# First norm of a decoder layer on one Trainium2 core: row tiles in groups of 2, 4, 4, 4 and 2, half of the squares of x on VectorE, a fifth buffer for raw rows

## The chip, the core and the metric

The kernel runs on one core of a Trainium2 chip. The core has five engines that work side by side, each through its own list of instructions in order, and they wait for each other by semaphores: TensorE (PE, matrix products; its weight loads are PEld), VectorE (DVE), ScalarE (ACT), GpSimd (POOL) and SyncE (SP, which here issues nearly all DMA transfers). The metric is the time of one execution on the device in microseconds, the median of some runs.

## The reference, cut to what matters

One decoder layer on x (512 tokens by 2048 features, fp32): a root-mean-square norm with a shift and scale made from a vector c, a wide projection, two groups of heads (retention, and sparse attention that selects keys by an indexer), an output projection with residual, and an MLP of four times the width behind a second norm. The part that the change touches:

```
def _rms_norm(x, g):
    y = xf * lax.rsqrt(jnp.mean(xf * xf, axis=-1, keepdims=True) + EPS)
    return (y * g.astype(jnp.float32)).astype(x.dtype)
...
    mod = jax.nn.silu(c) @ w_ada + b_ada          # 6 vectors of 2048; w_ada is 2048 x 12288
    shift1, scale1, gate1, shift2, scale2, gate2 = jnp.split(mod, N_MOD, axis=-1)
    h = _modulate(_rms_norm(x, norm1_g), shift1, scale1)   # h * (1 + scale) + shift
    proj = h @ w_in
    ...
    dk = _rms_norm(dk.reshape(B, L, DSA_KV_HEADS, HEAD_DIM), k_norm_g)
```

## The kernel before, in words

All activations lie transposed: a "row tile" kt is 128 features by 512 tokens, 16 of them make h. Every fp32 product is made of three passes over operands split into a high and a low half: ScalarE copies a piece of raw weights to `w_hi` (`split_hi`, L513), GpSimd subtracts to get `w_lo` (`split_lo`, L738), TensorE multiplies (`product`, L1194). Weights come in units of four chunks, numbered q = 4u + j, through two raw slots (`load_unit`, L448).

**Start.** x comes in four tiles of 128 tokens (1 MiB each) through the two halves of `x_nat`; tiles 2 and 3 are fetched when tiles 0 and 1 have been transposed and squared (L464 to L467). TensorE transposes them (`turn_x`), ScalarE copies them to `resid` and squares each with an accumulating sum (L660), all four squares on ScalarE. The four sums give the norm's factor through VectorE, a power on GpSimd (`root`, L747), a spread over partitions on TensorE (L1267) and a copy (L840).

**First norm and first projection.** Shift and scale for 4 row tiles are columns of `silu(c) @ w_ada`. They need 8 pieces of `w_ada` (`first_piece`, L455: 4 of scale, 4 of shift, each 4 x 128 rows by 512 columns, 1 MiB, rows of 2 KB) in four rotating buffers `first`; a piece t of group cc is issued when `first_used` has reached 8 cc + t - 3. TensorE takes a piece with `first_rows` (L1281, 4 products of 32 columns of the array each). After 8 pieces ScalarE copies the sum (`take_first`, L519), TensorE sums it (`sum_first`, L1302), VectorE adds the bias (L815), makes the gain (L820), and with ScalarE's part makes high and low of each row tile (`modulate`, L828 and L832, `h_high`, L523). With row tile kt ready, TensorE runs `early_chunk(kt)`: keys, values and three index tiles of the wide projection. There are four groups of 4 row tiles. In TensorE's order the pieces of group cc stand between the chunks of group cc - 1: none before the first, 4 before the second, 2 before the third, 2 before the fourth, whose middle holds `sum_first(cc)`; after the last pieces of all, chunk 11 to 15 follow.

**What SyncE issues behind that.** After the last piece: the unit of small projections (`U_SMALL`, unit 4); `ada_piece(0)`, which waits until all 32 first pieces have been used (L370); the store of the transposed x, 4 MiB, to `xT_dram` (L485); `ada_piece(1)`, which waits until that store has landed (L372); then unit 5 (`U_IQ`). `resid`'s memory is used again afterwards, so `take_kv` (VectorE, L889) waits for the store too: it takes keys and values of chunk 15 out of PSUM, and TensorE waits for it before its first narrow product of the small unit.

**The keys' norm.** `mean_square` (VectorE) makes the mean squares of the keys, GpSimd takes the power, which in its list stands behind `split_lo` of chunk 20, the first chunk of unit 5 (L767, L751), VectorE scales the keys (`scale_k`, L903), and TensorE transposes them behind the third chunk of the small unit (wait for `k_ready` at L1372).

Further on, pieces of `w_ada` for the other four vectors are summed on VectorE (L1013), and VectorE also adds the index scores (L925).

Of the kernel before, what the change touches and what calls it, by code (L numbers as in the profile page):

```python
# [98 lines left out]


def need(eng, sem, value):

    if isinstance(value, int) and value <= 0:
        return
    eng.wait_ge(sem, value)
# [20 lines left out]
def build(nc, x, vecs, b_ada, consts, w_ada, w_in, w_out, w_mlp1, w_mlp2, out):  # L126
# [21 lines left out]
    def small(name, *shape):  # L148
# [87 lines left out]
    x_turned, x_taken = sem("x_turned"), sem("x_taken")  # L236
    x_squared = sem("x_squared")
    rstd_spread = sem("rstd_spread")
# [117 lines left out]
    for n in range(2, ADA_PIECES):  # L356
        after = max(after, ada_place(n)[2] - 1)
        ADA_AFTER.setdefault(after, []).append(n)

    block = nc.Block()  # L360
    with block:
# [3 lines left out]
        def _(sp):  # L365
            def ada_piece(n):

                (sec, k), (b, _, freed) = divmod(n, 4), ada_place(n)
                if n == 0:
                    sp.wait_ge(first_used, 32)  # L370
                if n == ADA_EARLY[0]:
                    sp.wait_ge(xT_stored, 16)  # L372
                    sp.wait_ge(t_ready, KT)
                if n == ADA_LATE[0]:
                    sp.wait_ge(idx_done, len(ITEMS))
                need(sp, ada_added, freed)
                col = 2 * D + 512 * sec
                sp.dma_start(ada_rows[b][:], ada_v[:, 4 * k:4 * k + 4, col:col + 512]).then_inc(ada_landed[b], 16)
# [13 lines left out]
            def load_head(k):  # L392

                g = k // 4
                if k == 0:
                    sp.wait_ge(mod_taken, 8 + ADA_SUMS)
# [53 lines left out]
            def first_piece(cc, t):  # L450

                sec, s = divmod(t, 4)
                need(sp, first_used, 8 * cc + t - 3)
                col = D * (1 - sec) + 512 * cc
                sp.dma_start(first[t % 4][:].rearrange("p (k n) -> p k n", k=4),  # L455
                             ada_v[:, 4 * s:4 * s + 4, col:col + 512]).then_inc(first_landed[t % 4], 16)

# [48 lines left out]
        def _(act):  # L506
# [8 lines left out]
            def take_first(cc):  # L515

                act.wait_ge(first_used, 8 * cc + 8)
                need(act, mod_summed, cc)
                act.activation(part_rows[:], pa[:, 3, :], ACT.Copy).then_inc(first_taken, 1)  # L519

# [133 lines left out]
            for tb in range(NB):  # L654
                if tb == 1:
                    act.wait_ge(rows_taken, 2)
                    act.activation(csilu[:, 1, :], vec[:, V_C:V_C + KT], ACT.Exp, scale=-1.0).then_inc(silu_exp, 1)
                act.wait_ge(x_landed[tb % 2], 16 * (tb // 2 + 1))
                need(act, x_squared, tb)
                act.activation(x_junk[:], x_nat[:, tb % 2, :], ACT.Square,  # L660
                               accum_out=ms[:, tb:tb + 1]).then_inc(x_squared, 1)
                for q in range(4):
                    act.wait_ge(x_turned, 4 * tb + q + 1)
                    act.activation(resid[:, 4 * q:4 * q + 4, P * tb:P * tb + P],
                                   pj[:, q, :].rearrange("p (k t) -> p k t", k=4), ACT.Copy).then_inc(x_taken, 1)
            for cc in range(4):
                for j in range(4):
                    if cc > 0 and j == 2:
                        take_first(cc)
                    split_hi(cc, j)  # L670
                    if cc == 0:
                        if j == 0:
                            take_first(0)
                        h_high(j)
                    if cc > 0 and j == 2:
                        for m in range(4):
                            h_high(4 * cc + m)
            for q in range(Q_SMALL, Q_MLP):
# [100 lines left out]
        def _(dve):  # L779
            own = Steps(dve, dve_step)  # L780

            dve.memset(half[:], -0.5).then_inc(half_set, 1)
            own.step(dve.memset(c_wide[:], 0.0))
            dve.wait_ge(rows_turned, 1)
            dve.tensor_copy(bias_cols[:], pa[:, 0, 0:96]).then_inc(rows_taken, 1)
# [16 lines left out]
            def take_mod(n):  # L802

                col = 2 * KT + 4 * n
                dve.wait_ge(mod_summed, 4 + n + 1)
                dve.tensor_tensor(mod[:, col:col + 4], pa[:, 3, 0:4], bias_cols[:, col:col + 4],
                                  ALU.add).then_inc(mod_taken, 1)

            def take_first_mods(cc):

                dve.wait_ge(mod_summed, cc + 1)
                sums_ = pa[:, 3, 0:8].rearrange("p (m sec) -> p sec m", sec=2)
                for sec in range(2):
                    col = KT * (1 - sec) + 4 * cc
                    dve.tensor_tensor(mod[:, col:col + 4], sums_[:, sec, :], bias_cols[:, col:col + 4],  # L815
                                      ALU.add).then_inc(mod_taken, 1)
# [17 lines left out]

            for cc in range(4):
# [7 lines left out]
                dve.wait_ge(mod_taken, 2 * cc + 2)  # L843
                fold(4 * cc, 0, KT, V_N1, 4)
                for m in range(5):
                    kt = 4 * cc + m
                    if m < 4:
                        modulate(kt, 0, resid, rstd1[:], tmp1, 0, t_ready, h_hi, h_ready, 0)
# [151 lines left out]
            def ada_add(n):  # L1000
# [5 lines left out]
                if n % 4 == 0:  # L1006
                    dve.wait_ge(mod_summed, max(4, 3 + n // 4))
                for i in range(4):
# [10 lines left out]
            for q in range(Q_WO):  # L1019
# [35 lines left out]
                for n in ada_pieces_at(q):  # L1055
                    ada_add(n)
            dve.wait_ge(mod_taken, 8 + ADA_SUMS)
            fold(0, 1, 4 * KT, V_N2, KT)
# [131 lines left out]
        def _(pe):  # L1190
# [85 lines left out]

            def silu_rows(src, s, sec):

                for i in range(4):
                    at_ = 32 * (4 * s + i) + 1 - sec  # L1280
                    last = pe.matmul(pa[32 * i:32 * i + 32, 3, :], c_wide[:, at_:at_ + 32], src[i],  # L1281
                                     start=sec == 0 and s == 0, stop=sec == 1 and s == 3)
                return last

            def first_rows(cc, t):
# [8 lines left out]
                silu_rows([first[t % 4][:, 512 * i:512 * i + 512] for i in range(4)], s, sec).then_inc(first_used, 1)  # L1294

            def sum_first(cc):

                pe.wait_ge(first_taken, cc + 1)
                if cc == 0:
                    pe.wait_ge(c_wide_ready, 2)  # L1300
                for m in range(4):
                    last = pe.matmul(pa[:, 3, 2 * m:2 * m + 2], part_rows[:, P * m:P * m + P], pick[:],  # L1302
# [45 lines left out]
            fill(10)  # L1348
            for cc in range(1, 5):
                for s in range(4):  # L1350
                    if cc < 4:
                        for t in ((), (0, 1, 2, 3), (4, 5), (6, 7))[s]:
                            first_rows(cc, t)
                    early_chunk(4 * (cc - 1) + s, cc if cc < 4 and s == 3 else None)

            for j in range(4):
                pe.wait_ge(lo_done, Q_SMALL + j + 1)
                if j == 0:
                    pe.wait_ge(mod_taken, 8)
                for kk in range(4):  # L1360
# [17 lines left out]

            done = {"items": 0, "mods": 8, "heads": 0, "turns": 0}

# [335 lines left out]
```

## Time and profile before

| | us |
|---|---|
| median of 3 runs (2385.05 to 2387.38) | 2385.81 |
| profiled execution, its own time | 2386.79 |
| its span | 2385.0 |
| TensorE busy | 2347.0 (98%) |
| VectorE busy | 961.1 (40%) |
| ScalarE busy | 643.9 (27%) |
| GpSimd busy | 976.0 (41%) |
| mean granted TensorE clock | 0.994 |

The profile is one execution. Times in it run from the start of the span. A row of a timeline or of the chain of waits gives start and length. In brackets stands how long the engine sat idle before an instruction, and what ended that. In a table by stretch each engine has its busy time there (and its count of instructions), PEclk is the granted clock of TensorE as a share of its full 2.4 GHz (0.50 is 1.2 GHz), and the last two columns are the busy share of the 16 DMA engines and the GB/s that they moved.

### The profile page before, as it was taken

To read this page: it belongs to the slowest core of one execution; us is meant where nothing else is said; L and a number is where in the kernel's file an instruction comes from. 1 tells how busy PE (TensorE), PEld (TensorE's weight loads), DVE (VectorE), ACT (ScalarE), POOL (GpSimd) and SP (SyncE) were. 2 spreads that over 40 slices of the span, in tenths; PEclk is the share of its full clock that TensorE was granted. 3 is DMA by queue.
4 is the path that set the end of the run, shared out by engine and by line. 5 is a ranking of instruction groups with operands and counts; after the bars stand their busy time and mean duration, and the time that the engine had idled before them with its cause. 6 is when DMAs were issued, how large, how long until landed. Compare 5 with 4: busy or idle time off the path is not lost.

```text
span 2385.0 us, 26593 instructions
## 1 busy us (share of the span) xinstructions
PE 2347.0 (98%) x10744; PEld 1900.9 (80%) x10744; DVE 961.1 (40%) x1360; ACT 643.9 (27%) x891; POOL 976.0 (41%) x414
## 2 busy tenths in 40 slices
PE   6999999999999999999999999999999999999999
PEld 4676688788878888788888888888888888888887
DVE  2258898877866777621121121121121121121121
ACT  4222332223223221331222221221221221221222
POOL 1343243344434335344444444444444444444442
PEclk9999999999999999999999999999999999999999
DMA  9976455577647422223322322233223322332231
GB/s 379 358 275 227 159 172 181 194 252 278 242 146 266 158 89 81 76 92 105 106 102 75 106 106 92 84 106 106 90 85 106 106 85 91 106 106 81 96 128 49
DMA packets 183985, 342.13 MB, mean 143 GB/s; under 512 B 4417, under 2 KB 31332, under 8 KB 183012
## 3 DMA queue, kind: packets, MB, share of 16 engines
q1 hardware_dynamic: 175280, 336.77, 41.1%
q10 hardware_dynamic: 8628, 4.28, 0.6%
q8 instruction: 55, 0.90, 0.2%
q14 instruction: 22, 0.18, 0.0%
HBM read 324.26 MB, written 16.78 MB: 143 GB/s over the span
## 4 chain that ended last, share of the span: by engine, by line
PE 89%; DVE 5%; DMA 4%; issue 1%; ACT 1%; SPq 0%; POOL 0%; DVEq 0%; ACTq 0%
PE pj L1194 53%; PE pa L1194 31%; DMA ada_rows<-w_ada_in 2%; DVE part_rows L1013 2%; DMA ada_first<-w_ada_in 2%; DVE ada_acc L1013 2%; PE pa L1198 1%; PE pa L1281 1%; PE pa L1406 1%; PE pa L1447 1%; PE pa L1470 0%; DVE score L925 0%; PE pa L1274 0%; PE pa L1525 0%; PE pa L1517 0%
## 5 line engine op out<-in xcount | busy, mean ns | idle before, releaser
L738 POOL TENSOR_TENSOR w_lo<-raw,w_hi 128x1024 fp32r<-128x1024 f32 (+1 forms) x396 | 956.8, 2418 | 1349.6 <-ACT w_hi L513 1349.4
L513 ACT ACTIVATE w_hi<-raw 128x1024 fp32r<-128x1024 f32 (+1 forms) x396 | 416.2, 1054 | 1492.8 <-PE pj L1194 947.1
L1194 PE MATMUL pj<-h,w_hi 128*128 128x512 f32 (+1 forms) x1696 | 528.8, 393 | 4.0 <-DVE h L832 2.5
L1194 PE MATMUL pj<-w_hi,h 128*128 128x512 f32 x1408 | 454.1, 396 | 2.4 <-DVE rot L963 1.4
L1194 PEld LDWEIGHTS pj<-h,w_hi 128*128 128x128 f32 (+1 forms) x1696 | 316.4, 188 | 78.3 <-issue 10.7
L1194 PE MATMUL pa<-h,w_hi 128*128 128x512 f32 x1152 | 354.9, 389 | 0.0
L1194 PE MATMUL pj<-h,w_lo 128*128 128x512 f32 (+1 forms) x848 | 331.9, 391 | 0.0
L1194 PEld LDWEIGHTS pj<-w_hi,h 128*128 128x128 f32 x1408 | 264.3, 188 | 74.5 <-issue 14.7
L1194 PE MATMUL pa<-mid,w_hi 128*128 128x512 f32 x1024 | 316.1, 390 | 0.0
L1194 PE MATMUL pj<-mid,w_hi 128*128 128x512 f32 x1024 | 315.7, 390 | 0.0
L1194 PE MATMUL pj<-w_lo,h 128*128 128x512 f32 x704 | 274.4, 390 | 0.0
L1194 PEld LDWEIGHTS pa<-h,w_hi 128*128 128x128 f32 x1152 | 216.2, 188 | 45.0
L1194 PE MATMUL pa<-h,w_lo 128*128 128x512 f32 x576 | 224.1, 389 | 0.0
L1194 PEld LDWEIGHTS pj<-mid,w_hi 128*128 128x128 f32 x1024 | 191.8, 188 | 39.6
L1194 PEld LDWEIGHTS pa<-mid,w_hi 128*128 128x128 f32 x1024 | 191.6, 188 | 39.5
L1194 PE MATMUL pa<-mid,w_lo 128*128 128x512 f32 x512 | 199.3, 389 | 0.0
L1194 PE MATMUL pj<-mid,w_lo 128*128 128x512 f32 x512 | 199.3, 389 | 0.0
L1194 PEld LDWEIGHTS pj<-h,w_lo 128*128 128x128 f32 (+1 forms) x848 | 159.4, 188 | 34.5
L1181 DVE SCALAR_TENSOR_TENSOR resid<-pa,mod,resid 128x512 f32<-128x512 f32 x64 | 48.1, 751 | 304.0 <-PE pa L1194 304.0
L1181 DVE SCALAR_TENSOR_TENSOR resid<-pj,mod,resid 128x512 f32<-128x512 f32 x64 | 47.5, 751 | 276.8 <-PE pj L1194 276.8
L1194 PEld LDWEIGHTS pj<-w_lo,h 128*128 128x128 f32 x704 | 132.4, 188 | 27.4 <-issue 1.7
L1013 DVE SCALAR_TENSOR_TENSOR ada_acc<-ada_rows,csilu,ada_acc 128x512 f32<-128x512 f32 x120 | 129.1, 1076 | 27.2 <-DMA ada_rows<-w_ada_in 23.5
(172 smaller groups left out, 1684.9 us busy)
## 6 DMA issues: line engine op xcount, KB each, us to landing
raw<-w_mlp_in SPq DMA_DIRECT2D x64, 2048.0 KB, 8.6
ada_rows<-w_ada_in SPq DMA_DIRECT2D x64, 1024.0 KB, 5.2
raw<-w_in_in SPq DMA_DIRECT2D x22, 2048.0 KB, 10.1
ada_first<-w_ada_in SPq DMA_DIRECT2D x32, 1024.0 KB, 10.7
raw<-w_out_in SPq DMA_DIRECT2D x8, 2048.0 KB, 7.9
ret<-ret_dram SPq DMA_DIRECT2D x32, 256.0 KB, 3.9
raw<-w_in_in SPq DMA_DIRECT2D x3, 1792.0 KB, 12.8
x_nat<-x_in SPq DMA_DIRECT2D x4, 1024.0 KB, 10.1
```

The costliest lines, as they stand in the source:

```text
L513: act.activation(split_chunk(w_hi, u, j), raw_chunk(u, j), ACT.Copy).then_inc(hi_done, 1)
L738: pool.tensor_tensor(split_chunk(w_lo, u, j), raw_chunk(u, j), split_chunk(w_hi, u, j).bitcast(F32), ALU.subtract).then_inc(lo_done, 1)
L1013: last = dve.scalar_tensor_tensor(acc[:], ada_rows[b][:, i, :], c_col, acc[:], ALU.mult, ALU.add)
L1181: dve.scalar_tensor_tensor(resid[:, t, :], (pa if v % 2 else pj)[:, j, :], mod[:, 5 * KT + t:5 * KT + t + 1], resid[:, t, :], ALU.mult, AL ...
L1194: last = pe.matmul(dst, lhs[a], rhs[b], start=start and n == 0, stop=stop and n == 2)
L1198: return pe.transpose(dst, src, ident)
L1281: last = pe.matmul(pa[32 * i:32 * i + 32, 3, :], c_wide[:, at_:at_ + 32], src[i], start=sec == 0 and s == 0, stop=sec == 1 and s == 3)
L1406: pe.matmul(pa[:, n % 4, 0:span(i)], iqT[rows, hh // 2, P * i:P * i + P], ikT[rows, 0:span(i)], start=True, stop=True).then_inc(idx_done, 1)
L1447: last = pe.matmul(pa[:, bank, col:col + span(i)], qT[:, j, P * i:P * i + P], kT[:, g, 0:span(i)], start=True, stop=True)
```

## The change: what it does

The 16 row tiles of the first norm go in five groups of 2, 4, 4, 4 and 2. A piece of `w_ada` of the first and the last group has 256 columns, 0.5 MiB, in rows of 1 KB; there are 40 pieces. SyncE issues the pieces of the second group after quarter 1 of unit 0; TensorE takes two of them after chunk 0, six after chunk 1, and then its sum; from the third group on the pieces stand between the chunks of the group before, as they did. After the last piece chunks 13 to 15 follow. VectorE squares tiles 1 and 3 of x (tile 1 before it takes bias and vectors out of PSUM), ScalarE tiles 0 and 2. From the second group on, pieces 0 and 4 go to a fifth buffer, `first_again`, and the one they had lies where row tiles 12 and 13 of h are written. ScalarE's splits of a unit now stand ahead of `take_first` as a block of four. `ada_piece(0)` waits for all 40 pieces.

```diff
+GROUPS = ((0, 2), (2, 4), (6, 4), (10, 4), (14, 2))
+MODS = 2 * len(GROUPS)
...
+    x_junk2 = at("x_junk2", 8 * 4096, [P, D])
+    first_again = at("ada_first4", RC + 12288, [P, 2048])
...
+    def first_place(cc, t):
+        buffer = first_again if cc > 0 and t % 4 == 0 else first[t % 4]
+        return buffer[:, 0:4 * P * GROUPS[cc][1]].rearrange("p (k n) -> p k n", k=4)
...
-                    sp.wait_ge(first_used, 32)
+                    sp.wait_ge(first_used, 8 * len(GROUPS))
...
-                sp.wait_ge(x_squared, s + 1)
+                sp.wait_ge((x_squared, x_squared_too)[s], 1)
...
-            for j in range(1, 4):
-                load_quarter(j)
-            for cc in range(1, 4):
+            load_quarter(1)
+            sp.wait_ge(x_squared, 2)
+            for t in range(8):
+                if t == 4:
+                    load_quarter(2)
+                    load_quarter(3)
+                first_piece(1, t)
+            sp.wait_ge(x_turned, 16)
+            sp.wait_ge(x_squared_too, 2)
+            for cc in range(2, 5):
                 for t in range(8):
-                    if t == 4:
-                        if cc == 1:
-                            sp.wait_ge(x_turned, 16)
-                            sp.wait_ge(x_squared, 4)
-                        load_unit(cc)
+                    if t == 2:
+                        load_unit(cc - 1)
                     first_piece(cc, t)
...
-            for cc in range(4):
-                for j in range(4):
-                    if cc > 0 and j == 2:
-                        take_first(cc)
-                    split_hi(cc, j)
...
+            split_hi(0, 0)
+            take_first(0)
+            h_high(0)
+            split_hi(0, 1)
+            h_high(1)
+            split_hi(0, 2)
+            split_hi(0, 3)
+            for cc in range(1, 5):
+                if cc > 1:
+                    for j in range(4):
+                        split_hi(cc - 1, j)
+                take_first(cc)
+                for m in range(GROUPS[cc][1]):
+                    h_high(GROUPS[cc][0] + m)
...
+            dve.wait_ge(x_landed[1], 16)
+            dve.tensor_tensor_reduce(x_junk2[:], x_nat[:, 1, :], x_nat[:, 1, :], 1.0, 0.0, ALU.mult, ALU.add,
+                                     ms[:, 1:2]).then_inc(x_squared_too, 1)
...
+            square_x(3)
+            for cc, (kt0, count) in enumerate(GROUPS):
                 if cc == 0:
-                    dve.wait_ge(x_squared, NB)
+                    dve.wait_ge(x_squared, 2)
+                    dve.wait_ge(x_squared_too, 2)
...
-            for cc in range(1, 5):
-                for s in range(4):
-                    if cc < 4:
-                        for t in ((), (0, 1, 2, 3), (4, 5), (6, 7))[s]:
-                            first_rows(cc, t)
-                    early_chunk(4 * (cc - 1) + s, cc if cc < 4 and s == 3 else None)
+            early_chunk(0, None)
+            first_rows(1, 0)
+            first_rows(1, 1)
+            early_chunk(1, None)
+            for t in range(2, 8):
+                first_rows(1, t)
+            sum_first(1)
+            for cc in range(2, 5):
+                for m in range(4):
+                    for t in ((), (0, 1, 2, 3), (4, 5), (6, 7))[m]:
+                        first_rows(cc, t)
+                    early_chunk(GROUPS[cc - 1][0] + m, cc if m == 3 else None)
+            early_chunk(14, None)
+            early_chunk(15, None)
```

## Rows read from the trace of the kernel before

**Rows 1.** Stretches: length, busy PE, PEld, DVE, ACT, POOL; PEclk, DMA share, GB/s.

```profile
0.00:20.00 20.00, 8.90 (x58) 5.64 (x58) 2.28 (x12) 9.47 (x14) 0.20 (x4) 1.00 0.93 347
20.00:40.00 20.00, 14.63 (x98) 8.81 (x98) 0.86 (x2) 8.86 (x13) 3.09 (x2) 0.83 1.04 399
40.00:60.00 20.00, 17.24 (x106) 11.77 (x102) 11.51 (x11) 7.28 (x10) 8.71 (x4) 1.00 1.04 391
60.00:80.00 20.00, 17.59 (x94) 11.58 (x95) 6.08 (x10) 4.44 (x7) 5.19 (x3) 1.00 1.04 386
```

**Rows 2.** TensorE's timeline: pieces of w_ada (L1281) and the first chunk (L1194).

```profile
38.96 1.07 PE L1281 MATMUL pa<-ada_first,c_wide 128*32 128x512 f32 x8
...
44.74 0.50 PE L1194 MATMUL pj<-w_hi,h 128*128 128x512 f32 x1 [0.61 <-DVE h L832]
...
60.61 1.06 PE L1281 MATMUL pa<-ada_first,c_wide 128*32 128x512 f32 x8 [1.18 <-DMA ada_first<-w_ada_in]
63.32 1.07 PE L1281 MATMUL pa<-ada_first,c_wide 128*32 128x512 f32 x8 [1.65 <-DMA ada_first<-w_ada_in]
```

**Rows 3.** DMA queues over the whole span: packets, MB, share of 16 engines.

```profile
q1 hardware_dynamic: 175280, 336.77, 41.1%
q10 hardware_dynamic: 8628, 4.28, 0.6%
```

**Rows 4.** Groups by shape, VectorE, first 400 us: operations with two inputs.

```profile
L925 DVE SCALAR_TENSOR_TENSOR score<-stage,w_idx,score 128x512 f32<-128x512 f32 x15 | 11.5, 765 | 12.4 <-ACT stage L605 10.3 <-issue 1.0 <-DVE score L925 0.5
```

**Rows 5.** Chain of waits, 100 to 172 us: start, length, what.

```profile
105.76 3.01 PE pj L1194 x12
...
110.81 3.57 PE pa L1281 x32
...
129.71 0.80 PE pa L1302 x8
...
134.19 3.06 PE pj L1194 x12
...
139.29 2.72 PE pj L1194 x12
```

**Rows 6.** SyncE's timeline: the issues behind the last piece.

```profile
128.16 0.37 SPq L378 DMA_DIRECT2D ada_rows<-w_ada_in  x1
128.57 0.50 SPq L485 DMA_DIRECT2D xT_dram<-resid  x1
144.56 0.37 SPq L378 DMA_DIRECT2D ada_rows<-w_ada_in  x1
144.98 12.04 SPq L448 DMA_DIRECT2D raw<-w_in_in  x2
```

**Rows 7.** Tile raw, issue at 144.98 alone: time to its landing.

```profile
DMA to landing us min/median/max: 11.2/11.2/11.2
```

**Rows 8.** Timelines of VectorE, ScalarE, GpSimd, VectorE and TensorE around the keys.

```profile
149.60 0.42 DVE L894 COPY k_nat<-pj 128x256 f32<-128x256 f32 x1 [11.68 <-PE pj L1194]
...
159.12 1.06 ACT L513 ACTIVATE w_hi<-raw 128x1024 fp32r<-128x1024 f32 x1 [3.16 <-PE pj L1194]
...
160.26 2.93 POOL L738 TENSOR_TENSOR w_lo<-raw,w_hi 128x1024 fp32r<-128x1024 f32 x1 [3.63 <-ACT w_hi L513]
163.15 1.64 POOL L747 TENSOR_TENSOR ms<-ms,half 128x8 f32<-128x8 f32 x1
165.77 2.40 POOL L738 TENSOR_TENSOR w_lo<-raw,w_hi 128x1024 fp32r<-128x1024 f32 x1 [0.99 <-ACT w_hi L513]
...
164.82 3.83 DVE L903 TENSOR_SCALAR k_nat<-k_nat,ms 128x128 f32<-128x128 f32 x8 [3.89 <-POOL ms L747]
...
169.95 1.04 PE L1198 MATMUL pa<-con,k_nat 128*128 128x128 f32 x8
```

**Rows 9.** The same columns in stretches of 4 us.

```profile
228.00:232.00 4.00, 3.72 (x8) 1.30 (x7) 3.89 (x4) 0.31 (x2) 2.31 (x1) 0.62 0.00 0
232.00:236.00 4.00, 3.44 (x5) 1.66 (x6) 1.86 (x4) 0.95 (x2) 0.00 (x0) 0.50 0.60 189
```

More of the change, by code:

```diff
@@ L236, in build @@
     x_turned, x_taken = sem("x_turned"), sem("x_taken")
-    x_squared = sem("x_squared")
+    x_squared, x_squared_too = sem("x_squared"), sem("x_squared_too")
     rstd_spread = sem("rstd_spread")
@@ L395, in load_head @@
                 if k == 0:
-                    sp.wait_ge(mod_taken, 8 + ADA_SUMS)
+                    sp.wait_ge(mod_taken, MODS + ADA_SUMS)
                 elif k == 1:
@@ L453, in first_piece @@
                 need(sp, first_used, 8 * cc + t - 3)
-                col = D * (1 - sec) + 512 * cc
-                sp.dma_start(first[t % 4][:].rearrange("p (k n) -> p k n", k=4),
-                             ada_v[:, 4 * s:4 * s + 4, col:col + 512]).then_inc(first_landed[t % 4], 16)
+                col = D * (1 - sec) + P * GROUPS[cc][0]
+                sp.dma_start(first_place(cc, t),
+                             ada_v[:, 4 * s:4 * s + 4, col:col + P * GROUPS[cc][1]]).then_inc(first_landed[t % 4], 16)
             sp.dma_start(con[:, 0:P], consts[:, 0:P]).then_inc(const_landed, 16)
@@ L518, in take_first @@
                 need(act, mod_summed, cc)
-                act.activation(part_rows[:], pa[:, 3, :], ACT.Copy).then_inc(first_taken, 1)
+                width = P * GROUPS[cc][1]
+                act.activation(part_rows[:, 0:width], pa[:, 3, 0:width], ACT.Copy).then_inc(first_taken, 1)
             def h_high(kt):
@@ L658, in _ @@
                 act.wait_ge(x_landed[tb % 2], 16 * (tb // 2 + 1))
-                need(act, x_squared, tb)
-                act.activation(x_junk[:], x_nat[:, tb % 2, :], ACT.Square,
-                               accum_out=ms[:, tb:tb + 1]).then_inc(x_squared, 1)
+                if tb % 2 == 0:
+                    need(act, x_squared, tb // 2)
+                    act.activation(x_junk[:], x_nat[:, tb % 2, :], ACT.Square,
+                                   accum_out=ms[:, tb:tb + 1]).then_inc(x_squared, 1)
                 for q in range(4):
@@ L665, in _ @@
                                    pj[:, q, :].rearrange("p (k t) -> p k t", k=4), ACT.Copy).then_inc(x_taken, 1)
-            for cc in range(4):
-                for j in range(4):
-                    if cc > 0 and j == 2:
-                        take_first(cc)
-                    split_hi(cc, j)
[L671 to L677, printed above, removed]
+            split_hi(0, 0)
[12 more added lines that the diff above has]
+                    h_high(GROUPS[cc][0] + m)
             for q in range(Q_SMALL, Q_MLP):
@@ L811, in take_first_mods @@
                 dve.wait_ge(mod_summed, cc + 1)
-                sums_ = pa[:, 3, 0:8].rearrange("p (m sec) -> p sec m", sec=2)
+                kt0, count = GROUPS[cc]
+                sums_ = pa[:, 3, 0:2 * count].rearrange("p (m sec) -> p sec m", sec=2)
                 for sec in range(2):
-                    col = KT * (1 - sec) + 4 * cc
-                    dve.tensor_tensor(mod[:, col:col + 4], sums_[:, sec, :], bias_cols[:, col:col + 4],
+                    col = KT * (1 - sec) + kt0
+                    dve.tensor_tensor(mod[:, col:col + count], sums_[:, sec, :], bias_cols[:, col:col + count],
                                       ALU.add).then_inc(mod_taken, 1)
@@ L833, in modulate, with square_x @@
                                              h[:, kt, HI, :].bitcast(F32), ALU.add, ALU.subtract).then_inc(done, 1)
-            for cc in range(4):
+            def square_x(tb):
+                dve.wait_ge(x_landed[1], 16 * (tb // 2 + 1))
+                need(dve, x_squared_too, tb // 2)
+                dve.tensor_tensor_reduce(x_junk2[:], x_nat[:, 1, :], x_nat[:, 1, :], 1.0, 0.0, ALU.mult, ALU.add,
+                                         ms[:, tb:tb + 1]).then_inc(x_squared_too, 1)
+            square_x(3)
+            for cc, (kt0, count) in enumerate(GROUPS):
                 if cc == 0:
-                    dve.wait_ge(x_squared, NB)
+                    dve.wait_ge(x_squared, 2)
+                    dve.wait_ge(x_squared_too, 2)
                     dve.tensor_scalar(ms[:, 0:NB], ms[:, 0:NB], 1.0 / D, EPS, ALU.mult, ALU.add).then_inc(ms_ready, 1)
@@ L843, in _ @@
                 dve.wait_ge(mod_taken, 2 * cc + 2)
[L844 to L847, printed above, removed]
+                fold(kt0, 0, KT, V_N1, count)
+                for m in range(count + 1):
+                    kt = kt0 + m
+                    if m < count:
                         modulate(kt, 0, resid, rstd1[:], tmp1, 0, t_ready, h_hi, h_ready, 0)
@@ L1056, in _ @@
                     ada_add(n)
-            dve.wait_ge(mod_taken, 8 + ADA_SUMS)
+            dve.wait_ge(mod_taken, MODS + ADA_SUMS)
             fold(0, 1, 4 * KT, V_N2, KT)
@@ L1275, in sum_mod @@
                 last.then_inc(mod_summed, 1)
[L1277 to L1283, printed above, removed]
             def first_rows(cc, t):
@@ L1293, in first_rows @@
                     need(pe, mod_taken, 2 * cc)
-                silu_rows([first[t % 4][:, 512 * i:512 * i + 512] for i in range(4)], s, sec).then_inc(first_used, 1)
+                for i in range(4):
+                    at_ = 32 * (4 * s + i) + 1 - sec
+                    last = pe.matmul(pa[32 * i:32 * i + 32, 3, 0:P * GROUPS[cc][1]], c_wide[:, at_:at_ + 32],
+                                     first_place(cc, t)[:, i, :], start=t == 0, stop=t == 7)
+                last.then_inc(first_used, 1)
             def sum_first(cc):
@@ L1300, in sum_first @@
                     pe.wait_ge(c_wide_ready, 2)
-                for m in range(4):
+                for m in range(GROUPS[cc][1]):
                     last = pe.matmul(pa[:, 3, 2 * m:2 * m + 2], part_rows[:, P * m:P * m + P], pick[:],
@@ L1358, in _ @@
                 if j == 0:
-                    pe.wait_ge(mod_taken, 8)
+                    pe.wait_ge(mod_taken, MODS)
                 for kk in range(4):
@@ L1377, in _ @@
                         last.then_inc(k_turned, 1)
-            done = {"items": 0, "mods": 8, "heads": 0, "turns": 0}
+            done = {"items": 0, "mods": MODS, "heads": 0, "turns": 0}
             def bank3_free():
```

4 lines of the change are left out of this document (2 added, 2 removed).

## The prediction, made before the changed kernel was built or run

> **What bounds the kernel now.** The page comes first: TensorE is busy in 98% of the span, so only waits of TensorE, or work added to it, can move the end. The table by stretch says where its waits are [rows 1]: 20 - 8.90 = 11.1 us idle in the first stretch, then 5.4, 2.8 and 2.4 us. In the same four rows the DMA share is 0.93 to 1.04 at 347 to 399 GB/s. So up to 80 us the kernel is bound by transfers. TensorE's timeline shows it piece by piece [rows 2]: two pieces of 1 MiB start at 60.61 and 63.32, 2.71 us apart, each at its landing. The last piece of group 0 is used at 38.96 and chunk 0 starts at 44.74, 5.78 us later (copy, sum, bias, gain, high and low). The chain of waits shows the rest [rows 5]: from 105.76 to 134.19 nearly everything is TensorE's own, 28.43 us for 4 chunks, 8 pieces and a sum. Chunks 13, 14 and 15 begin at 139.29 with nothing between them; a chunk is 5.05 us behind pieces (110.81 - 105.76) and 4.76 behind another chunk, so they end near 153.6. Last, SyncE's timeline, which is no part of that chain but sets what comes behind it [rows 6].
>
> **1. Squares on VectorE.** VectorE's add on 512 elements with two inputs takes 765 ns [rows 4]; the trace has no square of 2048. Four of them are 3.1 us, the upper end; a start-up cost that is paid once and not four times would bring it nearer to 2.5, which I take. Tile 3 of x landed before four pieces and quarter 0 (448 KB, 1.2 us by bytes), at 38.96 - 4 x 2.71 - 1.2 = 26.9; two pairs of half pieces less ahead of it make that 22.5. Square, sum, power (1.64 [rows 8]), spread and copy bring the norm's factor to about 29 at the longer end, and its first use comes after 31. Cost: nothing at either end, the cover being some 2 us; without it each us would delay chunk 0. Nothing is gained either, since VectorE waited for the bias, not for the factor.
>
> **2. The first group of two.** Four MiB less lie ahead of its last piece: 4 x 2.71 = 10.8 us. Its rows are 1 KB instead of 2 KB. Packets of 496 B (4.28 MB / 8628) took 26.5 ns (0.6% of 16 x 2385 us), packets of 1921 B 89.5 ns [rows 3]. The line through both gives 50 ns for 1 KB, so 512 x 50 / 16 = 1.6 us for a half piece against 1.36 by bytes: 8 x 0.24 = 1.9 us back. The last piece lands at 38.9 - 10.8 + 1.9 = 30.0. The chain to chunk 0 is 5.78 less 1.1 for half the columns: chunk 0 at 34.7, 10 us earlier.
>
> The Trainium skill ("DMA: Bandwidth & Descriptors", Specifications) gives 512 B as the least transfer for line rate; by it the 1.9 us would be nothing and chunk 0 start at 32.8. The rows speak against it, and step 3 makes it worth nothing either way.
>
> **3. The second group.** Behind 30.0 come quarter 1 (1.2 us), four pieces (10.8), two quarters (2.4) and four pieces (10.8): 55.2. Piece 6 may be issued only when piece 2 is used, after chunk 1 (34.7 + 5.05 + 1.85 + 5.05 + 0.9 = 47.5), 5.0 us before its turn in the queue ends at 52.5: close, and a wait of up to 1 us there is in my bounds. So chunks 0 and 1 run from 34.7 to 46.6 and then TensorE takes a piece every 2.7 us. The last is used by 56.3, and its sum no longer lies within a chunk: copy 0.6, sum 1.05, VectorE and ScalarE 2.95 are all in the open. Chunk 2 starts at about 61.0; before it was 63.32 + 1.0 = 64.3. Of the 10 us gained 3.3 are left, plus two pieces (1.85) that are already used.
>
> **4. Third and fourth group.** Unit 1 (1792 KB, 4.7 us by bytes) now stands ahead of piece 2 of group 2, so its piece 3 lands at 55.2 + 5.4 + 4.7 + 5.4 = 70.7; TensorE wants it at 66.05 + 2.7 = 68.75: 1.9 us of waiting. The splits as a block ahead of `take_first` take GpSimd's work away from beside the gain, and with it 0.2 us that a group's chain took longer than chunk 3's rest (28.43 us for a group become 28.2). Chunk 2 takes until 66.05, the pieces with the wait until 71.6, chunks 3 to 5 with four pieces and a sum 19.5: chunk 6 at 91.1. A group of 28.2 follows: chunk 10 at 119.3. The last group's pieces have 256 columns: eight times 3.57 / 4 = 0.89 halved is 3.5 us less (bound: not halved, 3.5 us more than here), and the sum 0.4 less: chunk 14 at 119.3 + 24.3 = 143.6, the end of chunk 15 at 153.1. Before 153.6. **The whole early part is worth 0.5 us**: the transfers and TensorE's work are the same, and the wait has moved from ahead of chunk 0 to behind chunk 1.
>
> **5. What waits for the last piece.** This is what I think decides. Before, the last piece is used at 128.1, and chunk 15 ends 25.5 us later. Now chunks 13, 14, 15 follow it: 5.05 + 0.4 + 9.5 = 15.0 us. `ada_piece(0)` waits for it, and behind it in SyncE's list stand the store of x, then `ada_piece(1)` behind that store, then unit 5. Measured from the last use U [rows 6]: issues at U + 0.1 and U + 0.5, store landed at U + 16.4 (144.56 - 128.1); unit 4 lay ahead of it then. With a free queue 5 MiB are 13.5 us by bytes and the start of a transfer comes on top, so I take U + 15.1 to 16.4. Unit 5 is issued 0.4 later and lands 11.2 after that [rows 7]: U + 26.7 to 28.0. Before, there was room, since ScalarE took it at 159.12 = U + 31 [rows 8]. Now the chain is: high half 1.06, low half 2.40 to 2.93, the power 1.64, the scaling of the keys 3.83, with the handovers 9.1 to 9.6 us [rows 8]. Keys ready at U + 35.8 to 37.6. (Half of the 3.83 lay beside GpSimd's low half at 165.77; were it free of that, up to 2.4 us less, which is the bound below.) TensorE wants them, by its own work, 16.4 us after chunk 15 (169.95 - 153.6), at U + 31.4. **A wait of 4.4 to 6.2 us (2.0 at the bound below), I take 5.0**, where before the keys were there 1.3 us early (164.82 + 3.83 against 169.95). VectorE's `take_kv`, which was released by TensorE at 149.60, now waits for the store until U + 15.1 to 16.4 and takes 2.7 us; TensorE wants its result at U + 17.8. That is 0 to 1.3 us, within the wait for the keys. VectorE is late by the same 5 us, so no slack further on takes it back.
>
> **6. The clock.** It fell to half (1.2 GHz) in the stretch from 20 to 40 (PEclk 0.83) [rows 1], after TensorE had done single pieces with waits between, and again at 228 to 236 (0.62, 0.50) [rows 9], after waits for VectorE. The new kernel has a stretch of single pieces at 47 to 61 and a wait of 5 us near 170. Each may bring a fall: at the first chunk 2 comes up to 3 us late, of which the wait for piece 3 takes about 2; at the second half-rate work of up to 10 us loses up to 5. I put 0.5 and 1.7 in the sum. The Trainium skill ("TensorE: Matmul & The Clock Gate", HAM oscillation) tells of a kernel whose short bursts between DMA waits each started again at half clock; by it both falls would come.
>
> **Sum.** -0.5 + 0.5 + 5.0 + 1.7 = +6.7 us on the profiled execution's 2386.8, which stands 1.0 over the median of 2385.8: 2392.5 by the median.
>
> **Rivals.** (a) *The store's chain stays hidden.* If the store, unit 5 and GpSimd's power are done by U + 31.4, or the power does not wait for unit 5, nothing is added behind chunk 15, and the early part gives 0.5, or 2.5 where piece 3 of group 2 is not waited for: 2383.3 to 2385.3, not slower. For it: before, the store was 5.0 us early for `take_kv` (149.60 - 144.56). Against it: the last use moves 10.5 us nearer to the end of chunk 15, more than that room. It decides where 4.4 us are saved on that chain. (b) *Both falls of the clock in full*: +3 and +5 with the long end of the wait, 6.2: 2385.8 - 0.5 + 14 = 2399. For it the two falls of before; against it, waits downstream partly take them up. (c) *The first chunk doesn't start earlier*: the square of tile 1 stands ahead of what TensorE's pieces need (silu of c). Were it so long that pieces are used 10 us later, chunk 0 would start at 44.7 and all of group 1 shift, with the wait for keys: 2402. Against it: 3.1 us at most, begun when 2 MiB of x are there (5.4 us of transfer and some start), is over near 12, and the first pieces need silu of c only once they land, 1.6 us and more behind x.
>
> **Chances.** Forecast 0.62, (a) 0.2, (b) 0.14, (c) 0.04. The 8-in-10 range takes the bounds of the wait (2.0 to 6.2), of the early part (-2.5 to +3) and the clock (0 to 6): 2387 to 2399.5. A measurement here tells about 0.2%, 4.8 us, from no change: slower than that 0.65, within 0.27, faster 0.08.
>
> **What would show it.** Chunk 0 near 34.7 and chunk 2 near 61 (steps 2, 3); piece 3 of group 2 waited for near 70 (4); chunk 15 ending at 152 to 155; the store issued near 138.6 and landing at about 154, VectorE's L894 behind it; TensorE idle 4 to 6 us before its transposes of `k_nat`, with GpSimd's power behind a low half that waited for unit 5 (5). No such wait would prove me wrong, as would chunk 15 ending before 150.

## The result, and the profile after

The changed kernel took 2397.09 us (median of 6 runs, 2396.07 to 2397.93) against 2386.31 us for the kernel before (6 runs, 2385.05 to 2387.38): a ratio of 1.0046, 95% interval 1.0036 to 1.0056. It is **10.8 us slower**. The forecast was 6.7 us slower, 2392.5, with a range of 2387 to 2399.5. The profiled execution took 2397.9 us with a span of 2396.0.

The stretches of the changed kernel, in the columns of [rows 1]:

```profile
0.00:20.00 20.00, 8.68 (x68) 6.54 (x69) 4.50 (x14) 8.02 (x13) 0.20 (x4) 0.95 0.94 343
20.00:40.00 20.00, 18.89 (x134) 15.97 (x133) 7.81 (x11) 9.22 (x15) 5.23 (x3) 0.88 1.06 377
40.00:60.00 20.00, 15.01 (x93) 6.73 (x91) 0.00 (x0) 2.51 (x3) 4.20 (x2) 0.89 0.94 335
60.00:80.00 20.00, 17.15 (x82) 11.32 (x85) 6.14 (x11) 5.65 (x8) 6.29 (x3) 0.77 0.89 328
...
140.00:160.00 20.00, 19.10 (x97) 14.86 (x95) 5.74 (x15) 6.85 (x10) 7.91 (x4) 1.00 0.78 283
160.00:180.00 20.00, 14.03 (x60) 9.75 (x60) 10.43 (x30) 3.06 (x3) 8.61 (x4) 0.96 0.80 299
```

TensorE gained 4.3 us of work in the stretch from 20 to 40 and gave 2.2 back in the next. The new thing is the last row: 6 us idle between 160 and 180, where the kernel before had none, and a PEclk of 0.89 and 0.77 in the third and fourth, where it had 1.00.

TensorE's timeline, start, length and the idle time before, against [rows 2]:

```profile
35.30 0.50 PE L1226 MATMUL pj<-w_hi,h 128*128 128x512 f32 x1 [0.60 <-DVE h L855]
...
53.43 1.07 PE L1320 MATMUL pa<-ada_first,c_wide 128*32 128x512 f32 x8 [2.63 <-DMA ada_first<-w_ada_in]
56.14 1.94 PE L1320 MATMUL pa<-ada_first,c_wide 128*32 128x512 f32 x8 [1.65 <-DMA ada_first<-w_ada_in]
58.80 1.87 PE L1330 MATMUL pa<-pick,part_rows 128*128 128x2 f32 x8 [0.72 <-ACT part_rows L535]
63.52 0.80 PE L1226 MATMUL pj<-w_hi,h 128*128 128x512 f32 x1 [2.85 <-DVE h L855]
...
160.27 0.69 PE L1226 MATMUL pj<-h,w_hi 128*80 128x512 f32 x2 [1.18 <-DVE v_nat L927]
...
180.29 1.97 PE L1230 MATMUL pa<-con,k_nat 128*128 128x128 f32 x8 [5.98 <-DVE k_nat L935]
```

Chunk 0 starts 9.4 us earlier (35.30 for 44.74), chunk 2 at 63.52 where it began at 64.3. The last piece of group 1 and the sum take 1.94 and 1.87 us, where a piece and a sum took 1.07 and 1.05 before: the clock is at 1.2 GHz. Then, much later, comes a wait of 1.18 us for `take_kv`, and **5.98 us for the keys**, whose transposes come at 180.29 instead of 169.95.

The chain of waits (SPq is SyncE's queue; "issue" is time in which the engine waited for nothing that the profile shows) tells why, in order of time, and it is the one that was forecast; [rows 6 to 8] are its counterpart:

```profile
140.31 1.04 PE pa L1320 x16
...
141.37 0.37 SPq L389
...
141.79 15.66 DMA xT_dram<-resid
...
157.47 0.37 SPq L389
...
157.89 11.26 DMA raw<-w_in_in
...
169.23 1.07 ACT w_hi L528
...
170.36 2.40 POOL w_lo L757
172.77 1.61 POOL ms L766
...
174.40 0.05 DVE k_nat L935
174.45 2.23 issue
176.68 3.56 DVE k_nat L935 x7
...
180.29 1.97 PE pa L1230 x8
```

The last pieces are used at 141.35, the store of x is issued at 141.79 and lands 15.7 us later, then unit 5 comes, its high and low half, the power, the keys. VectorE's `take_kv`, too, is now released by the store and no longer by TensorE [rows 8]:

```profile
157.48 0.42 DVE L926 COPY k_nat<-pj 128x256 f32<-128x256 f32 x1 [10.77 <-DMA xT_dram<-resid]
```

In the kernel before, none of this lay on the chain.

### The profile page after: what moved, and what is told of

Same layout as the page of the kernel before. It is cut to its first block, busy times and chain, and to the rows that moved or that the text cites. A ratio compares the mean times of both kernels' runs of the same rounds, so it can differ in the third digit from the quotient of the medians.

```text
span 2396.0 us, 26739 instructions
## 1 busy us (share of the span) xinstructions
PE 2354.0 (98%) x10808; PEld 1909.9 (80%) x10808; DVE 953.9 (40%) x1367; ACT 641.0 (27%) x888; POOL 973.4 (41%) x414
## 4 chain that ended last, share of the span: by engine, by line
PE 93%; DVE 3%; DMA 2%; issue 1%; ACT 1%; POOL 0%; SPq 0%; ACTq 0%; DVEq 0%
PE pj L1226 56%; PE pa L1226 30%; PE pa L1320 1%; PE pa L1230 1%; DVE part_rows L1045 1%; PE pa L1442 1%; DMA xT_dram<-resid 1%; PE pa L1483 1%; DVE ada_acc L1045 1%; DMA x_nat<-x_in 1%; PE pa L1306 1%; PE pj L1230 1%; PE pa L1506 1%; DMA raw<-w_in_in 0%; DVE score L957 0%
## 5 line engine op out<-in xcount | busy, mean ns | idle before, releaser
L1045 DVE SCALAR_TENSOR_TENSOR part_rows<-ada_rows,csilu,part_rows 128x512 f32<-128x512 f32 x120 | 128.9, 1074 | 23.1 <-DMA ada_rows<-w_ada_in 19.3
```

Source lines behind the costliest of these rows:

```text
L1045: last = dve.scalar_tensor_tensor(acc[:], ada_rows[b][:, i, :], c_col, acc[:], ALU.mult, ALU.add)
```

## Experiments

Each was timed in interleaved rounds with the kernel before, whose median in the three sittings was 2386.3 to 2386.5 us. The theory of the prediction is called theory 1: the last piece is used nearer to the end of chunk 15, and with it the store, unit 5 and the keys come late.

### The late store alone, in the kernel before: three doses

Nothing but one wait is added; 12, 13 and 14 stand for the end of chunk 11, 12 and 13.

```diff
             load_unit(U_SMALL)
+            sp.wait_ge(chunk_used, 13)      # and 12, and 14, in the other two
             ada_piece(0)
```

> The kernel before, with one wait added: SyncE issues the first ada_rows piece, and so the store behind it, only when chunk 12 has been used (139.3 instead of 128.1), as late against the end of chunk 15 as the changed kernel has it. Nothing else changes. Theory 1: store lands near 155, unit 5 near 166.5, TensorE waits 5 to 6 us for the keys, perhaps with a fall of the clock: 2386.3 + 5 to 9, so 2391 to 2395 us. Rival: nothing hangs on it, 2386 to 2387 us.

> The kernel before, first ada_rows piece and store behind it held until chunk 11 has been used (134.2, 6.1 us later than 128.1; the kernel with chunk 12 had 11.2 us and cost 6.8). Theory 1 from rows: store lands near 150, unit 5 near 161.5, keys near 170.7, so TensorE waits 0.7 us, VectorE scales its keys 2 us later than before: 1 to 2.5 us, 2387.5 to 2389. A cost in proportion, without a threshold, would be 3.7 us: 2390.

> The same with chunk 13 (144.1, 16 us later). Theory 1: behind the threshold each us of delay is one of time, so 4.8 us more than with chunk 12: store near 160, keys near 181, TensorE waits some 10 us in all, 2396.5 to 2400 with a fall of the clock. Rival (the 6.8 us of the first dose were a fall of the clock or another accident): 2392 to 2395.

| held until the end of | later by (as planned) | median, us | ratio (95% interval) |
|---|---|---|---|
| chunk 11 | 6.1 | 2390.55 | 1.0022 (1.0013 to 1.0031) |
| chunk 12 | 11.2 | 2393.31 | 1.0031 (1.0019 to 1.0044) |
| chunk 13 | 16.0 | 2401.72 | 1.0068 (1.0054 to 1.0082) |

The middle dose puts the store about as late against the end of chunk 15 as the changed kernel has it. So this one late issue makes some 7 us of loss, with groups, squares and buffers as they were. The chunk 12 kernel's SyncE timeline and TensorE's waits (engine and line waited for, us, times, longest):

```profile
139.24 0.37 SPq L378 DMA_DIRECT2D ada_rows<-w_ada_in  x1
139.65 0.50 SPq L486 DMA_DIRECT2D xT_dram<-resid  x1
156.17 0.37 SPq L378 DMA_DIRECT2D ada_rows<-w_ada_in  x1
```

```profile
PE pj L1195 <- DVE v_nat L896: 2.7, 1, 2.7
PE pa L1407 <- DVE mod L807: 2.1, 1, 2.1
PE pa L1275 <- ACT stage L606: 1.9, 2, 1.6
PE pa L1199 <- DVE ik L887: 1.4, 1, 1.4
PE pa L1199 <- DVE k_nat L904: 1.2, 1, 1.2
```

The time was in the range expected, but the wait was not where I had put it. Only 3.9 us of it stand at `take_kv` and the keys. The rest comes later as waits for VectorE, at the index keys (`ik`) and at the sums for the gates (`mod`). The first dose cost 4.2 us where 1 to 2.5 were expected. I had worked it out from TensorE's wait for the keys, and its trace shows 0.35 us there, and 3.8 at the index keys:

```profile
173.34 1.09 PE L1199 MATMUL pa<-con,k_nat 128*128 128x128 f32 x8 [0.35 <-DVE k_nat L904]
...
200.49 1.11 PE L1199 MATMUL pa<-con,ik 128*128 128x128 f32 x4 [3.78 <-DVE ik L887]
```

This profiled execution was itself longer than the median (2394.64 us); its clock is at 0.83 from 60 to 80 and the store was issued at 137.37, later than the dose by itself would have it, so part of the 3.8 us in it may be the clock's.

VectorE has little idle time behind the keys (in the chunk 12 kernel it is busy for 19.4, 18.6 and 18.7 us in the three stretches of 20 us from 180 to 240), so what it gets late it hands on late. The third dose cost 15.4 us, above the 10 to 14 expected; 7.5 us of it stand at `take_kv`. Its profile is of the shortest of its five executions, 3.3 us under the median, so its waits explain 12 of the 15 us at best.

### The store ahead of the first gate piece, in the changed kernel

```diff
             load_unit(U_SMALL)
-            ada_piece(0)
             sp.wait_ge(x_taken, 16)
             sp.dma_start(xT_dram, resid[:]).then_inc(xT_stored, 16)
+            ada_piece(0)
             ada_piece(1)
```

> The changed kernel, with the store of x issued ahead of the first ada_rows piece, so that it no longer waits for the last of the 40 pieces. Theory 1 (the chain last piece, store, unit 5, low half, power, keys costs the time): the store is issued near 131 instead of 141.8 and lands near 152, unit 5 near 163 instead of 169.1, the keys are ready near 173 instead of 180.3; TensorE's idle 6.9 us between 140 and 180 shrinks to under 1, and with it the fall of the clock at 178: 2387 to 2390 us. Rival (the early part costs it: the clock's fall at 55 to 69 and the rearranged groups; the keys' wait is one that downstream slack would have taken up): 2394 to 2397 us.

Measured: 2390.03 us, ratio 1.0018 (1.0009 to 1.0027). That is 7 us of the 10.8 back, and the rival, 2394 to 2397, falls. TensorE no longer waits for the keys (their transposes begin at 173.02, which is 3.1 us later than in the kernel before, by the early part), but it waits for VectorE again further on:

```profile
PE pa L1230 <- DVE ik L918: 3.7, 1, 3.7
PE pa L1442 <- DVE mod L828: 2.1, 1, 2.1
```

SyncE's timeline shows what had stayed late: the store went out at 130.98, but behind the small unit, and unit 5 at 152.70, when the store had landed.

```profile
130.41 0.53 SPq L459 DMA_DIRECT2D raw<-w_in_in  x1
130.98 6.81 SPq L499 DMA_DIRECT2D xT_dram<-resid  x1
141.66 11.00 SPq L389 DMA_DIRECT2D ada_rows<-w_ada_in  x2
152.70 7.36 SPq L459 DMA_DIRECT2D raw<-w_in_in  x2
```

### The whole order of issues, then the unit, then the clock

Three kernels, each with one thing more than the last. The first: store, small unit, unit 5, then the gate pieces.

```diff
-            load_unit(U_SMALL)
-            ada_piece(0)
             sp.wait_ge(x_taken, 16)
             sp.dma_start(xT_dram, resid[:]).then_inc(xT_stored, 16)
+            load_unit(U_SMALL)
+            load_unit(U_IQ)
+            ada_piece(0)
             ada_piece(1)
```

> The changed kernel with another order of SyncE's issues behind the last pieces: store of x, small unit, unit 5, and only then the two ada_rows pieces. Theory 1, widened by what the store-first kernel showed (there unit 5 still landed at 163.9, VectorE had its keys 4.4 us later than before and TensorE then waited for VectorE at 198): the store lands near 147, unit 5 near 158 to 160, keys are scaled from 165 or 166, TensorE waits neither for keys nor for the index keys; what is left against before is the early part (chunk 15 ends near 156.4 against 153.6). 2387.5 to 2389.5 us. Rival (VectorE's lateness comes from something else than unit 5): as the store-first kernel, 2390.

Measured: 2389.46 us, ratio 1.0016 (1.0007 to 1.0025). The wait for the index keys goes from 3.7 to 1.1 us. Against the store-first kernel that is 0.6 us, which these intervals don't tell from nothing; of the two expectations neither is excluded by the time, though the waits are as the first had them.

The second: units 1 to 3 ahead of piece 4 again (`if t == 4:` for `if t == 2:`).

> As the kernel with the new order, and units 1 to 3 again issued ahead of piece 4 of a group, not ahead of piece 2. Piece 3 of group 2 then lands near 67 instead of 71.4. If the slow clock at 55 to 69 is what makes chunk 2 late, TensorE doesn't come to piece 3 before 71 anyway and nothing changes: within 0.5 us of the kernel with the new order. If the wait for piece 3 binds, up to 2 us less.

Measured: 2389.44 us, ratio 1.0015 (1.0006 to 1.0024): nothing.

The third adds small products on a zero tile.

```diff
+            def warm(count):
+                for _ in range(count):
+                    pe.matmul(pj[:, 0, 0:P], zeros[:], ident, start=False, stop=False, skip_group_check=True)
             for t in range(2, 8):
+                if t >= 6:
+                    warm(9 if t == 6 else 5)
                 first_rows(1, t)
+            warm(2)
             sum_first(1)
+            warm(9)
```

The tile's place and its zeroing are left out here.

> The last one with the 25 small products on a zero tile added, which keep the clock up between 48 and 61. In the kernel with these products alone the 3 us that chunk 2 gained were taken by the wait for piece 3 at 71.5, and the time stayed. Theory 2b (slow clock and piece 3 hide each other; only both together give the time back): chunk 3 starts near 69.5 instead of 74.8, chunk 15 ends near 151.5, 5 us under the kernel with the new order and some 2 under before, 2383 to 2386 us. Rival (transfers bind further on): chunk 15 ends at 154 or later and the time is 2386 to 2388.

Measured: 2387.01 us, ratio 1.0006 (0.9997 to 1.0015), level with the kernel before. The profile is of its shortest execution (2382.97), so only its stretches up to chunk 15 are compared here. Its clock stays up (PEclk stands behind the five engines):

```profile
40.00:60.00 20.00, 19.25 (x138) 11.51 (x131) 1.27 (x5) 2.59 (x4) 4.19 (x2) 1.00 0.96 347
60.00:80.00 20.00, 17.61 (x102) 10.57 (x101) 4.87 (x7) 6.33 (x8) 6.57 (x4) 1.00 1.05 391
```

But chunk 15 does not end at 151.5. Its last nine products begin at 151.25; nine such products took 2.04 us behind the chunk before, so it ends near 153.3, against 153.6 in the kernel before:

```profile
149.89 1.36 PE pj L1230 x6
151.25 4.80 PE pa L1230 x21
```

The time lies in the rival's range, 2386 to 2388, and not in that of 2383 to 2386. What bound was the transfers, as the rival had it: behind chunk 3, TensorE waits again for a piece of group 2.

```profile
77.79 1.06 PE L1324 MATMUL pa<-ada_first,c_wide 128*32 128x512 f32 x8 [1.65 <-DMA ada_first<-w_ada_in]
```

With every loss mended that the runs showed, two groups of two and a start 9 us earlier are worth 0.3 us at the end of chunk 15.

### The clock's first fall by itself

The same zero products, in the changed kernel as it is.

> The changed kernel, with products of a zero tile that TensorE adds to an open sum while it waits for the last two pieces of group 1 and for the first row tile behind them (25 small products, nothing computed changes). Theory 2 (the clock fell at 55.5 because TensorE did single pieces between waits, and chunk 2 ran at half rate): the clock stays at full rate from 40 to 80, chunk 2 takes 5.0 us instead of 7.7, its start moves from 63.5 to 61, and since the last piece moves with it everything behind is earlier: 2 to 3.5 us less, 2393.5 to 2395 us. If the wait for piece 3 of group 2 takes that up: under 1 us less. Rival (the fall has another cause): clock and time as they were, 2397.

Measured: 2397.89 us, ratio 1.0049 (1.0035 to 1.0062): no gain. In the profile the clock is at 1.00 from 40 to 60 and chunk 2 starts at 60.56, 3 us earlier, but then TensorE waits for pieces 2 and 3 of group 2:

```profile
60.56 0.50 PE L1228 MATMUL pj<-w_hi,h 128*128 128x512 f32 x1 [0.73 <-DVE h L857]
...
68.81 1.06 PE L1322 MATMUL pa<-ada_first,c_wide 128*32 128x512 f32 x8 [1.32 <-DMA ada_first<-w_ada_in]
71.52 1.94 PE L1322 MATMUL pa<-ada_first,c_wide 128*32 128x512 f32 x8 [1.65 <-DMA ada_first<-w_ada_in]
```

Piece 3 runs at half clock again (1.94 us). Of the 3 us some 0.8 are left at the last pieces, used at 140.54 for 141.35. The profile holds one thing more: the keys' transposes come at 177.30 there, 3.0 us earlier than in the changed kernel, with 1.2 us of waiting for them instead of 6.0. Yet the profiled execution is only 1.5 us shorter, and the median isn't shorter at all. TensorE waits 1.4 and 1.0 us for VectorE further on instead, at the index keys and at a gate sum, where the changed kernel waits for neither.

Together with the two kernels above: the earlier unit alone gives nothing, the warm clock alone gives nothing, both give 2.4 us (2389.44 to 2387.01). By the traces each hid behind the other. A full set of runs doesn't show it, since the clock by itself was tried only with the store still late, never with the new order of issues alone. The 2.4 us are the difference of two medians of one sitting, and the ratios' intervals just overlap; the first narrow products behind chunk 15 begin 2.0 us earlier in the trace (155.89 for 157.88). That the effect is there is likely, and its size is open by about 2 us.

### The clock's second fall by itself

```diff
                 if j == 2:
+                    fill(20)
                     pe.wait_ge(k_ready, 8)
```

> The changed kernel with 20 small products on the identity (5 us) that TensorE does while it waits for the keys, into a PSUM bank that is free then; nothing computed changes. The clock then stays at full rate from 178 to 185. If that fall costs what TensorE lost there (the transposes of the small unit came 12.6 us later than before, the keys 10.3): 2 to 2.5 us less, near 2395. Theory 1 as the store-first kernel refined it (VectorE, 5 to 9 us late by the keys, is the bound by 228): nothing, 2396.5 to 2397.5, since TensorE only waits longer for VectorE near 206 or 240.

Measured: 2396.49 us, ratio 1.0041 (1.0028 to 1.0055), the same as the changed kernel within the intervals. PEclk from 180 to 200 rose from 0.87 to 1.00. TensorE had that time to spare, since VectorE was by then the later of the two: it waits 2.1 us for a gate sum (`mod`) at 242.55, where the changed kernel waits for none.

### The squares alone, in the kernel before

```diff
+            dve.wait_ge(x_landed[1], 16)
+            dve.tensor_tensor_reduce(x_junk2[:], x_nat[:, 1, :], x_nat[:, 1, :], 1.0, 0.0, ALU.mult, ALU.add,
+                                     ms[:, 1:2]).then_inc(x_squared_too, 1)
...
-                act.activation(x_junk[:], x_nat[:, tb % 2, :], ACT.Square, ...)      # for all four tiles
+                if tb % 2 == 0:
+                    act.activation(x_junk[:], x_nat[:, tb % 2, :], ACT.Square, ...)
```

> The kernel before, with only the squares changed: VectorE squares x tiles 1 and 3, ScalarE 0 and 2. Both theories: no effect, since group 0 waits for its pieces and not for the norm's factor: 2385.5 to 2387 us. A rival would be that VectorE's squares delay silu of c and the pieces: +1 us or more, with chunk 0 later than 44.7.

Measured: 2386.29 us, ratio 0.9997 (0.9988 to 1.0006): nothing, as both theories had it. A square of 2048 takes VectorE 2.29 us.

### The order of issues alone, in the kernel before

> The kernel before with the new order of SyncE's issues alone. Before, the keys were ready 1.3 us early and VectorE idle 3.9 us ahead of them. Theory 1: the order frees nothing that TensorE waits for at 170, but VectorE has its keys up to 3 us earlier, and TensorE's waits for VectorE at 225 to 240 may shrink: 2383.5 to 2386.5 us. Rival: the ada_rows pieces, now behind unit 5, come too late for VectorE: 2387 to 2390.

The edit is the one shown for the order of issues. Measured: 2387.83 us, ratio 1.0008 (0.9999 to 1.0017). No gain. The time falls in the rival's range, 2387 to 2390, but the interval doesn't part it from no change, and TensorE's wait for a gate sum, where late gate pieces would show, is 0.9 us for 0.8. Why nothing came is clearer. VectorE still idles 3.9 us ahead of its keys, for GpSimd's power, because ScalarE takes chunk 20 at 159.08 whether unit 5 landed at 156 or, as here, at 148: that split waits for TensorE. I had expected a gain up to 3 us from an earlier landing, and missed that the landing was not what released the split.

## Why the prediction was right, and where its sizes were off

**Step 1, squares:** nothing, measured alone. 2.5 us were taken, 2.29 measured.

**Step 2, first group:** chunk 0 at 34.7 forecast, 35.30 measured: the last piece was used at 30.61 for 30.0, and the chain behind it took the 4.7 us of the forecast. Two half pieces that TensorE waited for one behind the other came 1.5 us apart (14.4 and 15.9), where 1.6 was drawn from the two queues [rows 3] and 1.36 is the time by bytes. So the rows of 1 KB did cost something, and a chunk 0 at 32.8, the time without that cost, is out.

**Step 3, second group:** chunk 2 at 61.0 forecast, 63.52 measured. The step was right about the transfers (the last piece was used from 56.14, forecast 55.2 to 56.3) and about the sum in the open. The clock, which step 6 had at up to 3 us with 0.5 in the sum, made the difference: with it kept up chunk 2 began at 60.56.

**Step 4, groups 3 and 4:** the end of chunk 15 was forecast at 153.1. The last pieces were used at 141.35 instead of 138.1, and TensorE reached its wait for `take_kv` 3.2 us later than by the forecast. This is **the term that was mis-sized**: the loss by the clock's first fall, put at up to 3 us, of which the wait for piece 3 of group 2 was to take about 2.

```profile
71.15 3.64 PE L1320 MATMUL pa<-ada_first,c_wide 128*32 128x512 f32 x32
74.72 0.50 PE L1226 MATMUL pj<-w_hi,h 128*128 128x512 f32 x1
```

Chunk 2 not only began 2.5 us late, it also took 7.6 us instead of 5.05, since most of it ran at half clock, and ended at 71.15 for 66.05: 5.1 us late. Piece 3 was there by its turn, so the 1.9 us of waiting for it fell away, as the step had it, and 3.1 us stayed: chunk 3 began at 74.72 for 71.6. With clock and unit position both mended chunk 15 ended at 153.3, so the early part without a fall of the clock is worth 0.3 us, where 0.5 was forecast.

**Step 5, what waits for the last piece:** confirmed link by link, but the last link was longer than its bounds. With U for the last use, 141.35, the store landed at U + 16.1 (15.1 to 16.4 forecast), unit 5 at U + 27.8 (26.7 to 28.0), keys ready at U + 38.9 (35.8 to 37.6). That is because GpSimd now had two low halves ready one behind the other, and the scaling of the keys took 5.83 us, not 3.83:

```profile
172.72 1.64 POOL L766 TENSOR_TENSOR ms<-ms,half 128x8 f32<-128x8 f32 x1
174.33 4.65 POOL L757 TENSOR_TENSOR w_lo<-raw,w_hi 128x1024 fp32r<-128x1024 f32 x2
...
174.40 5.83 DVE L935 TENSOR_SCALAR k_nat<-k_nat,ms 128x128 f32<-128x128 f32 x8 [9.40 <-POOL ms L766]
```

Forecast was a wait of 5.0; measured were 1.2 at `take_kv` and 6.0 at the keys, 7.2 in all, above the 4.4 to 6.2 of the step. Mending the order in the changed kernel gives 7.1 to 7.6 us back, making the store as late in the kernel before costs 7. What the step missed is that TensorE's wait for the keys and the time don't go together: in the kernel with the chunk 12 dose 2.7 of the 6.8 us stand behind the keys, as waits for VectorE, the first dose cost 4.2 us with 0.35 us of waiting for the keys in its trace, and in the changed kernel with the clock kept up 3.6 us less of waiting for `take_kv` and keys gave nothing in the median. How much VectorE's lateness costs by itself no run separates: of the 3.5 us that the store-first kernel was still slower, 3.1 can be the early part.

**Step 6, clock:** both falls came. PEclk is 0.89 and 0.77 in the two stretches from 40 to 80, where TensorE worked in short bursts between transfers. The Trainium skill ("TensorE: Matmul & The Clock Gate", HAM oscillation) tells of such bursts that each started again at half clock, and the trace agrees. Of the two prices, the first was 3.1 us at chunk 3 where I had 0.5 in the sum, and the second nothing, by its own experiment, where I had 1.7.

**Rivals:** (a), the chain hidden, is out by the 5.98 us wait; (c) is out by chunk 0 at 35.30; (b), both falls in full at 2399, overstated the second.

The sum as measured on TensorE at the keys: 3.2 (early part with the clock) + 1.2 + 6.0 make, before rounding, the 10.3 us of 180.29 - 169.95. The half clock behind that adds 2.3 us by the transposes of the small unit (194.48 for 181.86), part of it is taken up again further on, and the span ends 11.0 us later.

By the medians the loss of 10.8 us falls to 3.5 with the store first, 3.0 with the whole order of issues, and 0.5, which is not clear of noise, with the clock and the unit's place mended as well. Against the forecast's terms: the early part with its fall of the clock was put at nothing (-0.5 + 0.5) and cost about 3, the late chain was put at 5.0 and its waits are 7.2, the second fall was put at 1.7 and cost nothing. That the sum came as near as 4.1 us is in part luck, since this last term stood in for 1.7 us of the others.

## What to carry to other kernels

When the last use of a shared set of buffers moves towards the end of a stage, look at every issue that stands behind the wait for it in the DMA queue, and follow it through the other engines; here, four issues and three engines further on, it set TensorE's time, and there were 1.3 us of room. A start that comes earlier in a stretch bound by transfers only moves the wait: count the bytes up to the second use, not the first. Two small losses at one place can hide each other, so a repair that shows nothing alone may still count beside the other. A wait of TensorE that goes away gives its length back only where the engine it waited for isn't late at the next meeting too.

## What the runs showed of the hardware that was not expected

- VectorE's scaling of the keys, eight operations of 0.27 us (median), lengthened by 2 us for each of GpSimd's subtractions beside it: 3.77 to 3.83 us in the eleven profiles with one low half beside it (2.4 to 2.5 us), 5.83 and 5.85 us in the two with two in a row (4.65 us). The longest single operation took 2.4 us, as long as the subtraction beside it.
- The kernel before varied from 2382.5 to 2388.5 us over 33 runs, and in two groups: seven at 2382.5 to 2383.1, none from there to 2385.0, 26 above. Two profiled spans, 2385.0 (kernel before) and 2380.9 (squares alone, whose ratio is 0.9997), differ by the clock in the wait near 230: PEclk of 224 to 244 is 0.74 in one and 0.91 in the other. Two more profiles go the same way (0.91 with a span of 2381.2 in the kernel with everything mended, 0.74 with 2383.4 in the kernel before with the new order).

```profile
224.00:244.00 20.00, 17.66 (x54) 8.79 (x51) 11.47 (x15) 7.00 (x13) 2.65 (x1) 0.74 0.32 106
```

```profile
224.00:244.00 20.00, 17.55 (x64) 10.12 (x63) 14.52 (x17) 8.79 (x16) 4.99 (x2) 0.91 0.31 106
```

  A single profile is therefore worth some 4 us either way here, and differences under that were read from the medians.
